# Where VectorE normalises the attention rows: ahead of a step's filler work, or at the start of the next step

## The reference, cut to what matters

```python
def block(args):
    i, q_b, cq_b = args
    s = jnp.einsum('bqhd,bkhd->bhqk', q_b, k, preferred_element_type=jnp.float32) * (d ** -0.5)
    ...
    w = jax.nn.softmax(s, axis=-1).astype(v.dtype)
    return jnp.einsum('bhqk,bkhd->bqhd', w, v)
```

## Time and profile before

| | |
|---|---|
| median of 3 runs | 2364.12 us (2360.9 to 2365.56) |
| the profiled execution's own time | 2365.56 us |
| its span in the trace | 2363.8 us |
| granted TensorE clock, mean | 0.972 of 2.4 GHz |
| PE busy | 2250.5 us, 95% |
| DVE busy | 1260.1 us, 53% |
| ACT busy | 895.8 us, 38% |
| POOL busy | 346.2 us, 15% |
| swa and mla steps | about 52 to 255 us |
| fox steps | about 721 to 914 us |
| mem steps | about 1438 to 1501 us |
| dsa steps | about 1660 to 1751 us |

### The profile page before, as it was taken

The page is one execution under the profiler, slowest core; times in us unless marked ns, Lnnn a source line. Parts: engine busy times, 40 slices in busy tenths (PEclk is TensorE's granted clock), DMA queues, the critical chain, the costliest instruction groups (busy, mean ns, idle before and its releaser), DMA issues.

```text
span 2363.8 us, 28018 instructions
## 1 busy us (share of the span) xinstructions
PE 2250.5 (95%) x10188; PEld 1755.0 (74%) x10190; DVE 1260.1 (53%) x1955; ACT 895.8 (38%) x1475; POOL 346.2 (15%) x216
## 2 busy tenths in 40 slices
PE   7989899999999998899999989999989997999998
PEld 5756688888776776688888777568768775888886
DVE  4576653343464454553343575268489677443344
ACT  3544442243254444342242344322443343332333
POOL 0000510001320001500002430124023233000001
PEclk9999999999999999999999999879999998999999
DMA  6012133333233322233333233113212142323322
GB/s 169 18 37 76 50 102 98 98 97 101 68 91 94 95 81 63 66 104 107 89 98 98 89 91 104 36 45 111 83 58 72 36 116 63 98 82 114 89 72 71
DMA packets 360371, 196.69 MB, mean 83 GB/s; under 512 B 12593, under 2 KB 355390, under 8 KB 360271
## 3 DMA queue, kind: packets, MB, share of 16 engines
q1 hardware_dynamic: 360270, 195.36, 28.8%
HBM read 193.19 MB, written 2.14 MB: 83 GB/s over the span
## 4 chain that ended last, share of the span: by engine, by line
PE 85%; DVE 7%; ACT 3%; issue 3%; SPq 1%; DMA 0%; POOL 0%; DVEq 0%; ACTq 0%; POOLq 0%
PE PB L394 21%; PE PB L396 21%; PE PB L395 21%; PE PB L1333 3%; PE PB L1335 2%; PE PB L1334 2%; PE PB L476 2%; PE PB L522 2%; PE PB L495 2%; PE PB L1361 1%; PE PB L1414 1%; PE PB L1241 1%; PE PB L1242 1%; DVE WL L364 1%; PE PB L1247 1%
## 5 line engine op out<-in xcount | busy, mean ns | idle before, releaser
L358 ACT ACTIVATE WH<-RAW 128x1024 fp32r<-128x1024 f32 (+2 forms) x367 | 369.8, 1011 | 387.4 <-PE PB L396 359.3
L394 PE MATMUL PB<-XH,WH 128*128 128x512 f32 x1248 | 494.0, 396 | 12.6 <-DVE WL L364 7.1
L395 PE MATMUL PB<-XL,WH 128*128 128x512 f32 x1248 | 488.9, 392 | 0.0
L396 PE MATMUL PB<-XH,WL 128*128 128x512 f32 x1248 | 488.9, 392 | 0.0
L374 DVE TENSOR_TENSOR WL<-RAW,WH 128x1024 fp32r<-128x1024 f32 x192 | 252.3, 1314 | 186.7 <-ACT WH L358 177.0
L394 PEld LDWEIGHTS PB<-XH,WH 128*128 128x128 f32 x1248 | 235.6, 189 | 65.5 <-issue 12.7
L396 PEld LDWEIGHTS PB<-XH,WL 128*128 128x128 f32 x1248 | 235.5, 189 | 50.9
L395 PEld LDWEIGHTS PB<-XL,WH 128*128 128x128 f32 x1248 | 235.4, 189 | 48.3
L396 PE MATMUL PB<-HH,WL 128*128 128x512 f32 x512 | 199.2, 389 | 0.0
L394 PE MATMUL PB<-HH,WH 128*128 128x512 f32 x512 | 199.2, 389 | 0.0
L395 PE MATMUL PB<-HL,WH 128*128 128x512 f32 x512 | 199.2, 389 | 0.0
(11 more groups left out here) (508 smaller groups left out, 3663.0 us busy)
## 6 DMA issues: line engine op xcount, KB each, us to landing
RAW<-in_w_up SPq DMA_DIRECT2D x64, 512.0 KB, 4.1
RAW<-in_w_down SPq DMA_DIRECT2D x64, 512.0 KB, 3.8
RAW<-in_w_ffn_gate_up SPq DMA_DIRECT2D x44, 512.0 KB, 3.7
RAW<-in_w_gate SPq DMA_DIRECT2D x32, 512.0 KB, 3.8
RAW<-in_od_w_in SPq DMA_DIRECT2D x24, 512.0 KB, 6.4
RAW<-in_w_in SPq DMA_DIRECT2D x24, 512.0 KB, 3.8
RAW<-in_ple_w_gate SPq DMA_DIRECT2D x16, 512.0 KB, 3.9
RAW<-in_w_ffn_down SPq DMA_DIRECT2D x16, 512.0 KB, 3.9
```

The source lines that it names most:

```text
L358: act.activation(WH[:, s, 0:nb], RAW[:, s, 0:nb], ACT.Copy).then_inc(hi_done[s], 1)
L394: pe.matmul(PB[b][0:m, 0:n], WH[:, s, k, 0:m], rh[:, kk, :], start=kk == 0, stop=False)
L395: pe.matmul(PB[b][0:m, 0:n], WH[:, s, k, 0:m], rl[:, kk, :], start=False, stop=False)
L396: x = pe.matmul(PB[b][0:m, 0:n], WL[:, s, k, 0:m], rh[:, kk, :], start=False, stop=kk == last)
```

## The change

`dve_attend` normalised step c+1 ahead of `between(c)`. After the change it normalises step c at the start of step c, which is behind `between(c-1)` and ahead of `dve_max` of c+1. Nothing is added or removed: the same 160 pairs of reciprocal and product are issued, at another place of VectorE's list. No other engine's list changes.

```diff
             dve_max(dve, *steps[0])
             if start:
                 start()
-            dve_normalise(dve, *steps[0])
             for c, (kind, g, qb) in enumerate(steps):
+                dve_normalise(dve, kind, g, qb)
                 if c + 1 < len(steps):
                     dve_max(dve, *steps[c + 1])
                 if qb == 0 and c:
                     dve_out(dve, *steps[c - 1][:2])
-                if c + 1 < len(steps):
-                    dve_normalise(dve, *steps[c + 1])
                 between(c)
             if last:
                 dve_out(dve, *steps[-1][:2])
```

## The result

| | before | after |
|---|---|---|
| median, five runs each | 2363.95 us (2359.28 to 2365.56) | 2375.05 us (2373.72 to 2381.46) |
| ratio, 95% interval | | 1.0056 (1.004 to 1.0073) |
| span of the profiled execution | 2363.8 us | 2372.0 us |
| granted TensorE clock, mean | 0.972 | 0.979 |
| PE busy | 2250.5 us | 2238.6 us |

Two things in this table don't fit a story of stalls alone: the mean clock is *higher* after, and TensorE's busy time is 12 us *smaller* with the same list.

A forecast was written before the change was run, and what follows sets the result against it. TensorE's list plus its idle gaps was taken as the bound. Swa and mla 21.1, fox 4.7, mem 6.2, dsa -3.1 and lower clock 6.3 sum to 35.2 us on the 2364.12 median: forecast 2399, range 2379 to 2416.

The forecast's parts named there:

- the rule of the two times: Each step: compare when TensorE reaches the transposes of c with when VectorE finishes `between(c-1)`, which the normalise now follows.
- step 7 with its clock: Swa and mla, first chain: filler starts 6.45 us late, net 4.95 lost, plus 1.8 of lower clock.
- step 10 with its clock: Swa and mla, second chain: filler 5.5 us late, 1.3 comes back, net 4.2, plus 1.8 of lower clock.
- steps 11 to 31 with the clock of step 31: Swa and mla: 12 losses of 16.6 us less 6.9 of vanished waits, net 9.7, plus 1.8 of lower clock.
- fox: Query block 3 of the seven pairs with projections: transposes end 0.67 us late each, 4.7 in all.
- mem with its clock: Mem attention: delays of 3.05, 2.0 and 1.2 us at steps 1 to 3, sum 6.2, plus 0.9 of lower clock.
- dsa: Dsa attention: a gain of 3.1 us, as the splits of tiles 10 and 11 come before TensorE wants them.
- the clock: Lower TensorE clock behind new idles: 5.4 us for steps 7, 10 and 31, 0.9 in mem, together 6.3.
- The recoveries: Swa and mla, steps 11 to 31: waits disappear where VectorE's `between` starts earlier, giving back 6.9 us.
- the "cheaper" rival: Only steps 7, 9, 10, fox and mem cost; earlier `between` absorbs steps 11 to 31: 18.7 us, 2383; chance 0.12.
- The "dearer" rival: Stalls feed each other and the lower clock follows shorter stalls too: about 2414, with cascades 2420; chance 0.17.
- The rival "same": New idle is taken from later waits, some 35 us of them not shifting with TensorE: 2364; chance 0.04.

The follow-up runs named there:

- table_early: The kernel before, with ScalarE's tanh table load moved to the start of head product 7 of the index stage: 2346.86 us, ratio 0.9945.
- after_table: The whole change plus the earlier table load of table_early: 2375.10 us, ratio 1.0052 to the kernel before, 28.2 slower than table_early.
- late_mixer: The kernel before with the normalise moved only in the swa and mla stretch (32 of the 72 steps): 2384.85 us, ratio 1.0105.
- late_mem: The kernel before with the normalise moved only in the mem attention (8 steps): 2352.25 us, ratio 0.9968.
- table_gain: table_early with the normalise moved in dsa and at steps 12, 15, 16, 27, 28 of swa and mla, 30 of fox, 4 of mem: 2343.55 us.
- table_mid: table_early plus the moved normalise in steps 11 to 31 of the swa and mla stretch alone: 2354.65 us, 7.8 above table_early.
- table_chains: table_early plus the moved normalise in steps 7 and 10 of the swa and mla stretch alone: 2357.79 us, 10.9 above table_early.
- shift12: The kernel before with 12 extra 128x512 matmuls ahead of the first index product: 2367.14 us; 12 executions at 2362.6 to 2370.0, 2 at 2347.4 and 2348.5.

## Why the prediction was right or wrong

**The mechanism and the direction.** Right. Each of the stalls was where the rule of the two times put it: transposes of TensorE against the end of `between` on VectorE. By the traces they came out as follows (clock behind the wait included; for the swa and mla steps the copies of after against those of table_early, for the rest the ledger or the experiment named).

| term | forecast | measured |
|---|---|---|
| steps 1 to 6 | 0.5 | 0.0 |
| step 7 with its clock | 4.95 + 1.8 | 6.2 |
| step 9 | 1.75 | 1.2 |
| step 10 with its clock | 4.2 + 1.8 | 5.9 |
| steps 11 to 31 with the clock of step 31 | 9.7 + 1.8 | 9.9 |
| fox | 4.7 | 4.4 |
| mem with its clock | 6.2 + 0.9 | 5.9 |
| dsa | -3.1 | -1.6 to -2.6 |
| sum | 35.2 | 31 to 32 by these, 28.5 by the ledger (31.6 without the loss of before at the entry of fox), 28.2 or 26.7 by the medians |
| index stage | not in the sum | -18.1 by the ledger, -13.8 by the medians (table_early) |

**The step that failed** is "the clock" in the sum. It counted the lower clock only behind waits that the change makes or takes away. It took for fixed what the clock does behind waits that stay, and the largest such stretch of the kernel, 50 us at half clock behind a wait of 1.01 us, was no term at all, neither in the sum nor in the range. With that term at its measured value, 13.8 to 18.1, the sum is 17.1 to 21.4 and the time 2381 to 2386, inside the range. The experiments show both halves of this: with the wait taken out (table_early against after_table) the change costs 28.2; with the wait kept, the stalls of one stretch alone cost 24.2 (late_mixer, half clock), and those of mem alone made it 8.4 faster (late_mem, full clock).

**What would have shown it.** I wrote that an unchanged span with the waits of line 600 there would mean that later slack takes them. It was the right watch for the wrong reason: the stalls of line 600 are there, and no later wait took them. The mean clock of the whole run (0.979 after, 0.972 before) said it at once.

**Smaller misses.** The 3 to 9 between 35.2 and these sums are sizes. The normalise takes 0.9 to 1.0 when both exponentials are there, not 1.21, and it stood in nearly every term. The first head's transposes start before the second head is ready. Step 14 lost 0.3 where I had 1.65. The other large middle steps had the sizes forecast: TensorE waits 2.37, 1.23, 1.46, 0.96, 2.16 and 3.29 at steps 13, 21, 23, 25, 26 and 31, where I had losses of 2.75, 1.45, 1.8, 1.45, 2.05 and 3.3. In dsa I missed that the normalise of step 7 would itself come 2.8 late.

The clock fell behind two of these that I had left out (granted 0.51 from 152.00 to 155.50 behind step 13, 0.50 from 234.00 to 237.40 behind step 26), and no longer behind the waits for the rotation and for VT, which it had done before (154.0 to 157.4, 222.3 to 225.7); the two pairs cancel.

**The recoveries** came, but not for the reason that I gave. I had waits disappear "where VectorE's `between` now starts earlier". table_gain made `between` start earlier at those steps alone, and gained nothing. The waits shrank because a stall a step or two ahead had made TensorE late for them: with step 26 late, the wait of 3.2 for VT is 1.5 in table_mid, and with step 26 in time it stays 3.2 (table_gain, table_chains). For the two small matmuls that waited for a rotation (0.73 and 1.49) this wasn't tried. It follows that the "cheaper" rival, which let steps 11 to 31 be absorbed by such an earlier start, was wrong too, though its time (2383) was the nearest of all: the middle steps cost 9.9. The "dearer" rival had two parts. That stalls feed each other isn't seen: the middle steps cost 9.9 behind the chains and 12.7 alone. That the lower clock follows shorter stalls came in part, behind 2.37, 2.16 and the 2.65 of mem, but not behind those of 0.96 to 1.88; it has no net cost in the middle steps, and 1.7 in mem, where I had 0.9.

**The rival "same"** asked for 35 us of waits behind the attentions that don't shift with TensorE. I looked for waits and found none; a stretch at low clock is a reserve of the same kind, and is no wait.

**Open.** What decides whether the clock falls behind the 1.01 us wait. It goes with how much work stands ahead, but by no single bound: 4.6 us of added work turn it in 15 of 16 executions, 2.8 us in 2 of 14, and about 19 us (1499.25 to 1518.25 at the last step of mem), in late_mixer, in none of 6; with 28 (1527.11, the changed kernel) the profile has full clock. No rule that I could test came out of this. That it needs the wait is shown; which outcome another shift would have is not, and neither is what an execution carries from its start to the wait.

## What to carry to other kernels

Before you sum stalls, read the granted clock along the whole span: a stretch at the lower level that begins behind a short wait can turn over when anything ahead of it shifts by a few microseconds, so it belongs in the range, and it is worth more to remove that wait than to order the work around it. Compare an edit with such a stretch held fixed (here by one table load moved a few microseconds, which alone is worth 13.8 us, half of what the whole change cost), or the price of the edit comes mixed with that of the clock. A recovery behind a loss can be the loss paid back, as those that were tried here were; try the recovering steps alone before you count on them.

## What the runs showed of the hardware that I had not expected

- A wait of 1.01 us cost 50 us at half clock; behind waits of 5.91 and 3.4 us the clock was back about 4 us after their end. In the index stage it came back only at 1570.6, 5 us behind the last ReLU of a head product. Why it stayed low so long there was not tried.
- One kernel has two times: 2347 to 2349 and 2363 to 2370 (shift12), by the mean clock, and by the clock of one stage where there is a profile.
- Added work made the kernel faster: 20 matmuls, 4.6 us, gave 2353 against 2361.
- The table load of 1.28 us makes TensorE wait for nothing when it falls into an idle stretch of ScalarE, ahead of the ReLU of product 7 (1505.12 in table_early) and not behind that of product 8.
